# A gated DeltaNet mixer put in another order inside a two-layer fp32 trunk on one Trainium2 core

## The reference, cut to what matters

```
for l in range(2):
    h = swiglu_ffn(rms_norm(x, g), w_in, w_out);  x = x + 0.5 * rms_norm(h, g)
    h = rms_norm(x, g) @ mix_w_in                # columns: q k v z (4 heads x 128), a b (4 each), 2 x 512 gated
    o_gdn = delta_rule(silu(conv4(q,k,v)), g(a), beta(b)) -> rms_norm over the head * silu(z)
    u = causal_conv31(h1 * sigmoid(h2)) + bias;  o_cm = silu(layer_norm(u))
    x = x + rms_norm(concat(o_gdn, o_cm) @ mix_w_out, g)
    h = swiglu_ffn(...);  x = rms_norm(x + 0.5 * rms_norm(h, g), g)
```

## Time and profile before

| what | value |
|---|---|
| median of 3 runs | 2207.22 us (2206.28 to 2208.68) |
| the profiled execution | 2205.52 us, its span 2203.8 us |
| PE busy, share of the span | 2099.9 us, 95% |
| DVE busy | 1239.1 us, 56% |
| ACT busy | 682.8 us, 31% |
| mean granted clock of PE | 0.967 |
| first mixer | about 382.5 to 719 us from the span's start |
| second mixer | about 1465 to 1801 us |

### The profile page before, as it was taken

The page is one execution under the profiler, slowest core; times in us unless marked ns, Lnnn a source line. Parts: engine busy times, 40 slices in busy tenths (PEclk is TensorE's granted clock), DMA queues, the critical chain, the costliest instruction groups (busy, mean ns, idle before and its releaser), DMA issues.

```text
span 2203.8 us, 26235 instructions
## 1 busy us (share of the span) xinstructions
PE 2099.9 (95%) x10044; PEld 1756.1 (80%) x10044; DVE 1239.1 (56%) x1707; ACT 682.8 (31%) x914; POOL 38.9 (2%) x51
## 2 busy tenths in 40 slices
PE   7999999997988999999999999999979799999997
PEld 6888887875887788888788888878758778888886
DVE  5555422899855755542375554258988656555323
ACT  5222222434225422222242222233341343222222
POOL 0000000000010000000000000000010000000000
PEclk9999999998999999999999999999979999999997
DMA  5333333223001233333233333323220023333320
GB/s 160 104 95 95 98 95 93 77 77 86 1 1 58 77 99 99 97 87 97 84 96 96 95 93 97 97 67 92 81 58 1 1 67 100 99 97 93 96 79 39
DMA packets 345792, 177.54 MB, mean 81 GB/s; under 512 B 8338, under 2 KB 344692, under 8 KB 345716
## 3 DMA queue, kind: packets, MB, share of 16 engines
q1 hardware_dynamic: 344058, 176.34, 28.0%
q10 hardware_dynamic: 1658, 0.16, 0.1%
HBM read 174.38 MB, written 2.10 MB: 80 GB/s over the span
## 4 chain that ended last, share of the span: by engine, by line
PE 77%; DVE 17%; ACT 3%; issue 2%; DMA 0%; DVEq 0%; SPq 0%; ACTq 0%
PE res L457 21%; PE res L459 21%; PE res L458 21%; DVE u L1301 7%; DVE cacc L1385 2%; PE res L521 1%; PE res L522 1%; PE pq L692 1%; PE stat L464 1%; PE res L525 1%; DVE wl L1137 1%; PE bc L485 1%; DVE pre L1371 1%; PE pq L457 1%; PE pq L459 1%
## 5 line engine op out<-in xcount | busy, mean ns | idle before, releaser
L818 ACT ACTIVATE wh<-raw 128x1024 fp32r<-128x1024 f32 (+1 forms) x336 | 347.8, 1037 | 1014.0 <-PE res L459 993.1
L1137 DVE TENSOR_TENSOR wl<-raw,wh 128x1024 fp32r<-128x1024 f32 (+1 forms) x336 | 401.8, 1197 | 392.6 <-ACT wh L818 392.2
L457 PE MATMUL res<-xh,wh 128*128 128x512 f32 x1576 | 614.2, 390 | 3.0 <-DVE xl L1151 3.0
L458 PE MATMUL res<-xl,wh 128*128 128x512 f32 x1576 | 613.2, 389 | 0.0
L459 PE MATMUL res<-xh,wl 128*128 128x512 f32 x1576 | 613.2, 389 | 0.0
L457 PEld LDWEIGHTS res<-xh,wh 128*128 128x128 f32 x1576 | 295.8, 188 | 65.0 <-DVE wl L1137 2.5
L459 PEld LDWEIGHTS res<-xh,wl 128*128 128x128 f32 x1576 | 295.8, 188 | 61.6
L458 PEld LDWEIGHTS res<-xl,wh 128*128 128x128 f32 x1576 | 295.8, 188 | 61.2
L457 PE MATMUL res<-hh,wh 128*128 128x512 f32 x704 | 273.9, 389 | 0.0
L458 PE MATMUL res<-hl,wh 128*128 128x512 f32 x704 | 273.9, 389 | 0.0
L459 PE MATMUL res<-hh,wl 128*128 128x512 f32 x704 | 273.9, 389 | 0.0
(11 more groups left out here) (268 smaller groups left out, 1936.1 us busy)
## 6 DMA issues: line engine op xcount, KB each, us to landing
raw<-in_ffn_w_in SPq DMA_DIRECT2D x176, 512.0 KB, 3.8
raw<-in_ffn_w_out SPq DMA_DIRECT2D x64, 448.0 KB, 3.7
raw<-in_mix_w_in SPq DMA_DIRECT2D x48, 512.0 KB, 4.0
raw<-in_ffn_w_out SPq DMA_DIRECT2D x32, 512.0 KB, 3.8
raw<-in_mix_w_out SPq DMA_DIRECT2D x16, 512.0 KB, 3.9
xin<-in_x SPq DMA_DIRECT2D x4, 512.0 KB, 5.0
out_dram<-xin SPq DMA_DIRECT2D x4, 512.0 KB, 4.0
crows<-in_cm_dw_w ACTq DMA_DIRECT2D x1, 62.0 KB
```

The lines of the kernel that those rows point to most:

```text
L457: pe.matmul(bank, wh[:, slot, j, :], hi, start=first, stop=False)
L458: pe.matmul(bank, wh[:, slot, j, :], lo, start=False, stop=False)
L818: act.activation(wh[:, slot, 0:nk, :], raw[:, slot, 0:nk, :], ACT.Copy).then_inc(hi_full, 1)
L1137: dve.tensor_tensor(wl[:, slot, 0:nk, :], raw[:, slot, 0:nk, :], wh[:, slot, 0:nk, :].bitcast(F32), ALU.subtract).then_inc(lo_full, 1)
```

## The change

In the mixer the order is now K, V, Q (units 0 to 11), the gated units (12 to 19) one by one between the chunk steps, Z (20 to 23) tile by tile in the scan. The chunk matrices move to the region of the FFN's hidden values, so x stays readable. Factors are merged: K is no longer copied, scaled and transposed back; the mask goes on `QK` (POOL) and 1/length of k squared times beta on `Dm`; q's length goes into the epsilon of the output norm. The first tap of the 4-tap convolution moves from DVE to ACT. The convolution's taps all come after the first gated tile. The layer norm of the convolution moves behind the scan, and the heads' half of `mix_out` comes first. Outside the mixer, `spread` at a stage's end is followed by 12 products that nobody reads, and `x_sums` and `spread` inside `first_units` come later.

```diff
+                if q % 2:
+                    for n in range(IDLE_PRODUCTS):
+                        pe.matmul(in_bank(4)[:, 0:P], ident[:], ones[:], start=True, stop=True)
...
-                    if k == KD - 3 and not two:
-                        x_sums(stage, l)
...
+                for n in (4, 5):
+                    pe.wait_ge(lo_full, l * UNITS + (u0 + n + 1 + SLOTS))
+                    for k in range(KD):
+                        if n == 4 and k == (3 if two else 0):
+                            x_sums(stage, l)
+                        if (n, k) == ((5, 0) if two else (4, 2)):
+                            spread(stat_q, l)
+                        mm = tile(in_bank(n), n - 4, k, xh[:, k, :], xl[:, k, :], k == 0, k == KD - 1)
+                    mm.then_inc(unit_done, 1)
```

PE's order in the mixer after `first_units` (units 0 to 5). The transposes and products between the units are those of before (V, K, K'K, K'Q, T), without the one of `Um`:

```diff
+                unit(6)
+                unit(7)
                 pe.wait_ge(wab_ready, l * 2 + 2)
+                pe.wait_ge(rs_ready, l * 3 + 2)
...
+                unit(8)
+                unit(9)
...
+                unit(10)
+                unit(11)
+                unit(12)
...
+                pe.wait_ge(l2_sq, l * 2 * H + 2 * H)
+                for n in range(2 * H):
+                    for c in range(NC):
+                        mm = pe.matmul(bc[:, n * NC + c:n * NC + c + 1], ksq[:, n, c * P:(c + 1) * P],
+                                       ones[:, 0:1], start=True, stop=True)
+                mm.then_inc(l2_full, 1)
...
+                decays(0)
+                decays(1)
+                unit(13)
+                decays(2)
+                decays(3)
+                unit(14)
...
+                unit(15)
...
+                unit(16)
...
+                unit(17)
...
+                unit(18)
...
+                unit(19)
```

ACT for each of the 12 K, V, Q units (`abT` is the block of the a and b columns, which PE turns between units 9 and 10):

```diff
+                for r in range(NQKV):
+                    which = (1, 2, 0)[r // H]
+                    w0 = C_QKV + which * H + r % H
+                    act.wait_ge(mix_free, l * MIX_IN_U + r + 1)
+                    act.activation(cacc[:, r % 2, :], pre[:, 0:T], ACT.Copy,
+                                   scale=call[:, l, w0:w0 + 1]).then_inc(tap0_ready, 1)
                     if r > 2:
                         high(MBASE + r + SLOTS, r % SLOTS, 8, l)
...
+                    act.wait_ge(cv_ready, l * NQKV + r + 1)
+                    dst = (kT, vT, qT)[r // H][:, r % H, :]
+                    act.activation(dst, cacc[:, r % 2, :], ACT.Silu).then_inc(act_kvqz, 1)
+                    if r // H != 1:
+                        act.wait_ge(act_kvqz, l * 4 * H + r + 1)
+                        act.activation(ksq[:, r if r < H else r - H, :], dst, ACT.Square).then_inc(l2_sq, 1)
+                    if r == 8:
+                        act.wait_ge(abT_full, l + 1)
+                        act.activation(abT[:], bc[0:2 * H, :], ACT.Copy).then_inc(abT_ready, 1)
```

DVE for the same units:

```diff
+                def qkv_unit(r):
                     dve.wait_ge(unit_done, l * UNITS + (MBASE + r + 1 + SLOTS))
+                    if r:
+                        dve.wait_ge(cv_ready, l * NQKV + r)
+                    dve.tensor_tensor(pre[:, PADG:], in_bank(mix_bank(r, l)), rs[:], ALU.mult).then_inc(mix_free, 1)
+                    if r > 2:
+                        weight_low(MBASE + r + SLOTS, r % SLOTS, 8, l)
+                    which = (1, 2, 0)[r // H]
+                    dve.wait_ge(tap0_ready, l * NQKV + r + 1)
+                    for k in range(1, GTAPS):
+                        at0 = C_QKV + k * 3 * H + which * H + r % H
+                        if k > 1:
+                            st.need(mark)
+                        ins = dve.scalar_tensor_tensor(cacc[:, r % 2, :], pre[:, k:k + T], call[:, l, at0:at0 + 1],
+                                                       cacc[:, r % 2, :], ALU.mult, ALU.add)
+                        if k < GTAPS - 1:
+                            mark = st.done(ins)
                         else:
+                            ins.then_inc(cv_ready, 1)
```

DVE behind the Q units, from unit 13 on, with every call of `conv_taps`. The operations left out between the calls are those of before (`vb`, `Bm`, `pm` and the odd columns of `Um`, `QK`, four each); the six levels follow with `conv_taps(2)` four times in each:

```diff
+                glu_unit(13)
+                glu_tile(0)
+                conv_taps(2, 1)
+                glu_unit(14)
...
+                conv_taps(4, 1)
+                glu_unit(15)
+                conv_taps(1, 1)
+                glu_tile(1)
+                conv_taps(6, 2)
+                glu_unit(16)
+                conv_taps(2, 2)
...
+                glu_unit(17)
+                conv_taps(1, 2)
+                glu_tile(2)
...
+                conv_taps(4, 3)
+                glu_unit(18)
+                conv_taps(4, 3)
+                glu_unit(19)
+                conv_taps(1, 3)
+                glu_tile(3)
```

DVE in the scan, `for c in range(NC)`; the last lines stand behind the output of block c:

```diff
+                    if c >= 2:
+                        z_unit(c - 2)
+                    else:
+                        conv_taps(3)
...
+                    if c == 1:
+                        conv_taps(CT * CTAPS)
+                        for t in range(CT):
+                            st.need(tap_mark[t])
+                        dve.sem_inc(u_ready, 1)
+                    if c == 2:
+                        dve.wait_ge(usum_full, l + 1)
+                        dve.tensor_scalar(rcol[:], stat[:, 0:NC], 1.0 / CW, None, ALU.mult).then_inc(mu_ready, 1)
```

PE in the scan and behind it (the wait for `u_ready` stands in block 2, behind its four tiles of Z):

```diff
+                    z_tiles(2)
...
+                    z_tiles(4)
...
+                        pe.wait_ge(u_ready, l + 1)
+                        for t in range(CT):
+                            mm = token_sums(u[:, t, :], first=t == 0, last=t == CT - 1)
+                        mm.then_inc(usum_full, 1)
+                z_tiles(4)
+                pe.wait_ge(mu_ready, l + 1)
+                spread_column(rcol).then_inc(mubc_full, 1)
+                z_tiles(4)
+                for t in range(CT):
+                    pe.wait_ge(usq_ready, l * CT + t + 1)
+                    mm = token_sums(glu[:, t, PADC:], first=t == 0, last=t == CT - 1)
+                mm.then_inc(vsum_full, 1)
```

More of the change, by code:

```diff
@@ L357, in _ @@
                 w_mix = mix_w_in.rearrange("l (k p) c -> l p k c", p=P)
+                with sp.Fori(0, 2) as i:
+                    for h in range(H):
+                        load(i * 4 + (MBASE + h), h, w_mix[l, :, :, bass.ds(i * (V0 - K0) + (K0 + h * P), P)], l)
+                for h in range(H):
+                    load(MBASE + 2 * H + h, h, w_mix[l, :, :, h * P:(h + 1) * P], l)
                 with sp.Fori(0, CT // 2) as i:
@@ L361, in _ @@
                         col = i * (2 * P) + (G0 + (q // 2) * P + (q % 2) * CW)
[L362 to L366, removed]
+                        load(i * 4 + (MBASE + NQKV + q), q, w_mix[l, :, :, bass.ds(col, P)], l)
+                for h in range(H):
+                    load(MBASE + Z_U + h, h, w_mix[l, :, :, Z0 + h * P:Z0 + (h + 1) * P], l)
                 w_mo = mix_w_out.rearrange("l (k p) c -> l p k c", p=P)
@@ L598, in _, with unit @@
                 first_units(MBASE, 1, 2, l)
[L600 to L605, removed]
+                def unit(r):
+                    pe.wait_ge(mix_free, l * MIX_IN_U + mix_need(r, l))
+                    in_unit(MBASE + r, r % SLOTS, mix_bank(r, l), l)
+                unit(6)
+                unit(7)
                 pe.wait_ge(wab_ready, l * 2 + 2)
+                pe.wait_ge(rs_ready, l * 3 + 2)
                 for k in range(KD):
@@ new lines, in _ @@
+                pe.wait_ge(udiag, l + 1)
+                spread_column(rcol).then_inc(uvbc_full, 1)
+                def mix_out(m, half):
+                    for k in range(CT):
+                        if m == 0:
+                            pe.wait_ge(cmix_ready if half else gm_ready, l * H + k + 1)
+                        hi, lo = (hic, loc) if half else (hig, log)
+                        mm = tile(res[:, m % 4, :], m % SLOTS, half * CT + k, hi[:, k, :], lo[:, k, :],
+                                  half == 0 and k == 0, half == 1 and k == CT - 1)
@@ L979, in _ @@
+                high(MBASE + 12 + SLOTS, 0, 8, l)
+                act.wait_ge(l2_full, l + 1)
+                act.activation(gt["ss"][:, 0:16], bc[:, 0:16], ACT.Sqrt, bias=eps[:, 0:1]).then_inc(l2_root, 1)
                 act.wait_ge(gc_full, l + 1)
@@ L1016, in _, with z_gate @@
                                        res[:, 2 * g:2 * g + 2, :], ACT.Copy).then_inc(u_upd, 1)
+                def z_gate(n):
+                    high(MBASE + Z_U + n + SLOTS, n, 8, l)
+                    act.wait_ge(mix_free, l * MIX_IN_U + Z_U + n + 1)
+                    act.activation(zT[:, n, :], zT[:, n, :], ACT.Silu).then_inc(act_kvqz, 1)
                 for c in range(NC):
@@ L1526, in _ @@
[L1526 to L1530 removed]
+                        dve.tensor_tensor(on[:, :, c, :], oq[:], four(res[:, 3, :]), ALU.add).then_inc(o_free, 1)
```

497 lines of the change are left out of this document (207 added, 290 removed).

## The result

The changed kernel takes 2267.8 us (median of 4 runs, 2267.3 to 2269.0) against 2206.75 for the kernel before: ratio 1.027, 95% interval 1.026 to 1.029, 61 us slower. Predicted were 2249 (2224 to 2268).

The account below looks back on a forecast made before the run. DVE was taken to set the mixer's pace up to 542 us, PE the FFNs' and projection's. Each mixer 24 us longer (28 ahead, 30 and 22 lost): 2205.5 + 48 - 6 = 2247.5 profiled, median 2249, range 2224 to 2268.

Parts of the forecast that it names:

- cold idle products: Rival at the stage boundaries: the clock has fallen before every spread, so savings go; 2264 us, 12% chance.
- The piece of 45: Behind block 1's output, before block 2's Xd: 45 leftover taps take 29.8 us and PE waits 28.2 us.
- K, V, Q units: Mixer, 412.1 to 483.3: a chain through ACT sets 6.3 us a unit, 5.9 behind a V unit; sum 71.2 us.
- The 15% rival, units at PE's rate: K, V, Q units: ACT's chain is shorter, units 3 to 11 take 5.44 us; kernel 2229 us, 15% chance.
- Start of the stage: Mixer's beginning: idle products take 2.9 us and hold the clock; DVE takes unit 0 at 412.1 instead of 414.0.
- To the levels: Mixer, 483.3 to 553.9: length products 8.5 us, then PE is the chain; sum 70.6 us.
- Levels to the scan: Mixer, 553.9 to 610.0: six doubling levels with eight taps each, 9.38 us a level; 56.1 us.
- Scan and tail: Mixer from 610.0 on: leftover taps, blocks, Z's units, output norm and projection take 132.6 us.
- Boundaries: In front of the FFNs: three boundaries save up to 2.9 us each, 2 taken for one; 6 us saved.
- The drain behind a table load: ACT function changes: a drain of about 1.38 us each, two on a mixer's path; 2255 us, 3 in 100.
- The covered taps: Rival at the piece behind block 1: it costs PE nothing, each mixer 28 us shorter, kernel 2193 us; 6% chance.

Follow-up runs that it names:

- Experiment 1: The changed kernel without the 45 convolution taps behind block 1's output (result incomplete): 2205.2 us, 62.6 less.
- experiment 3: The changed kernel with tap 0 of the K, V, Q units back on DVE and the next weight's split behind the taps: 2226.4 us.
- experiment 5: The changed kernel with only the next weight's split moved behind the three taps, tap 0 still on ACT: 2234.1 us.
- Experiment 2: The changed kernel with K's length products moved into PE's wait before the transposes of abT: 2253.8 us.
- experiment 6: The changed kernel with both the split behind the taps and K's length products before the transposes of abT: 2231.2 us.
- experiment 7: Experiment 6 with 12 of the 45 taps moved into the levels: 2219.1 us.
- experiment 9: Experiment 3 with gated tile 0's two units ahead of K, V, Q and 30 of the 45 taps placed earlier: 2190.5 us, ratio 0.992.
- experiment 12: Experiment 9's order with taps moved twice more by the traces, 3 left behind block 1's output: 2170.2 us, ratio 0.982 to the kernel before.
- Experiment 11: The kernel before with only the 12 idle products added behind the spread in front of each of five stages: 2215.4 us, ratio 1.004.

## Why the prediction was right, and where it was short

The side and the mechanism were right. That the time, 2267.8, lies inside the range is in part luck: the edge is 0.2 us away, the loss was 61 us where 42 were added up, and the range reached so far because of cold idle products, which are not what made it long. By its own steps, on the clock of the old trace (after's first mixer runs 1.28 later):

- **The piece of 45.** Counted from the diff, 29.8 us predicted, 29.90 measured; PE's wait 28.2 and 28.54. Experiment 1 shows what it costs, 62.6 us. That this is the loss to within 2 us is a coincidence of several terms: experiments 3 and 5 take 41 and 34 us from the same kernel without touching the piece, so what the new order gained elsewhere and what the units cost happen to cancel.
- **K, V, Q units.** 6.3 and 5.9 us predicted; 6.38 and 6.00 measured. The 15% rival, units at PE's rate, is out. Experiments 3 and 5 show the chain: with the split moved behind the taps it opens. PE's wait before the transposes of `abT` was 9.5 instead of 12, since PE itself came later: it had waited 3.26 us for a split (the 3.3 in the table of waits), which the prediction did not have. The last taps ended at 486.2 instead of 483.3, of which 1.4 came from the start.
- **Start of the stage.** DVE's first pre came at 413.5 instead of 412.1. The clock fell already in the spread (2.08 us instead of the earlier trace rows's 1.16), and the idle products took 3.52 instead of 2.9.
- **To the levels.** 70.6 predicted, 76.7 measured. This is the term that was mis-sized: the one-column products. I took 0.136 us a record from the earlier trace rows, and 8.5 in all; they took 13.81, 0.216 each. The row was no price of either level: it counts weight loads, and the clock fell in the middle of it (1.00 up to 551, 0.75 in 551 to 552, then 0.50). Experiment 2 shows both prices, 0.113 and 0.218. The clock fell once more in front of the products (0.64 in 488:490) and stayed at 0.50 to 509; the 2.5 us that the prediction had set down for the clock in this stretch went to the decays and the unit behind them. So the first pm of the levels came 16 us earlier than before and not 26.
- **Levels to the scan.** 56.1 predicted, 57.7 measured.
- **Scan and tail.** 132.6 predicted, 132.3 measured.

2.9 + 6.1 + 1.6 - 0.3 is 10.2 before rounding: the first mixer is 34.2 us longer and not 24. The second is 29.9 longer, with the same waits. Two places make up most of the 4.3 between them, and both are the clock: its start is 1.5 us shorter (spread 1.16, idle products 2.84), and from block 2's Xd to block 3's it takes 14.95 us instead of 17.12. There the 32 sums over u took 3.63 us, in the first mixer 4.82.

- **Boundaries.** 6 us predicted as saved; the three stages behind them are 0.8, 1.3 and 1.8 shorter, 3.9 together. The 1.3 by which the first mixer comes later lie in the first FFN and are no boundary: the clock was 0.88 in 10:20 where the kernel before had 1.00, and in experiments 6 and 7, with the same order there, this stage took 379.1 us as before. The idle products took 2.84 us in front of the second mixer alone and 3.52 to 4.47 in front of the other four stages: the clock mostly fell inside them. The 12% rival, cold idle products, is half true, then. It had the clock fall before the spread at every boundary, and 15 us more; that happened at one (the first mixer, 2.08 us), and without the products the kernel is 7.5 us slower.

Sum: 34.2 + 29.9 + 1.3 - 3.9 = 61.5, where 42 were predicted.

- **The drain behind a table load,** the 3% case of 2255: the changed kernel shows none either. Its load at 502.98 takes 1.28 us, and the next activation starts at 504.27.
- **The covered taps.** "DVE idles 2 us in each of the K, V, Q units" was the right observation on the rival's side. Experiments 9 and 12 turn it into a kernel: the taps need one finished gated tile, and two units moved ahead give it.

## What to carry to other kernels

When work of one engine is background for another, count it by place, not by sum: an order that brings forward what has no background work leaves the engine idle there and collects the rest in one piece elsewhere. Count the instructions from the source; the size of such a piece can then be told to a per cent. In a chain that goes back and forth between two engines, look first at what stands in front of the dependent step: one split moved behind three taps was worth 34 us here. And price a product at the clock it will find: behind PE's longer waits that was the low one here, at nearly twice the time. After each edit read the waits again: a move worth 14 us was worth nothing when another edit had taken the wait. And before a difference of 2 or 3 us is put down to an edit, look in which stage of the trace it lies; here it was once a stage that the edit did not touch.

## What the runs showed of the hardware

- In experiments 3, 5 and 9 the 64 one-column records came right behind full units and still took 10.5 to 10.9 us, between 7.3 (twice experiment 2's 3.63) and 13.81: the clock fell within the run, with PE busy all the time (experiment 3: 1.00 in 472:474, 0.77 in 474:476, then 0.50). Experiment 11 shows the step, 8 records in 0.95 us and 8 later ones in 1.71.
- POOL slows DVE by the kind of operation: taps with both inputs in SBUF went from 0.70 (two in 1.40) to 0.8 to 1.4 beside products and sums (two in 1.61 to 2.81), and to a mean of 1.08 over the eight of which QK's mask met the first half; operations with an input in PSUM stayed at 0.69.
- Beside a working DVE a product by a scalar column on POOL takes 1.56 to 1.88 us for 128x512, a sum 1.26 to 1.65; DVE's combined tap alone is 0.66.
- The clock can fall at different places in kernels with the same waits (experiment 11), and even in the two mixers of one kernel (3.63 and 4.82 us for the same 32 sums over u); 5 us hang on it. I know no row of the kernel before that tells where.
